# First level of the blockwise inverse in the delta stage: products with the identity become transposes

## What is computed

```python
a_mat = jnp.where(tri_strict, jnp.einsum('bhncd,bhnsd->bhncs', kb, k) * decay, 0.0)
t_mat = a_mat + jnp.eye(C, dtype=a_mat.dtype)
u = lax.linalg.triangular_solve(t_mat, vb, left_side=True, lower=True, unit_diagonal=True)
w = lax.linalg.triangular_solve(t_mat, kb * jnp.exp(g)[..., None], left_side=True, lower=True,
                                unit_diagonal=True)
qk = jnp.where(tri_incl, jnp.einsum('bhncd,bhnsd->bhncs', q, k) * decay, 0.0)

def step(S, xs):
    q_c, k_c, u_c, w_c, qk_c, g_c = xs
    v_new = u_c - jnp.einsum('bhcd,bhde->bhce', w_c, S)
    o = jnp.einsum('bhcd,bhde->bhce', q_c * jnp.exp(g_c)[..., None], S) + jnp.einsum('bhcs,bhse->bhce', qk_c, v_new)
    g_last = g_c[..., -1]
    S = S * jnp.exp(g_last)[..., None, None] + jnp.einsum(
        'bhcd,bhce->bhde', k_c * jnp.exp(g_last[..., None] - g_c)[..., None], v_new)
    return S, o
```

## Time and profile before

| | |
|---|---|
| median of 3 runs | 6135.12 us (6133.20 to 6140.82) |
| span of the profiled execution | 6134.8 us |
| the delta stage in it | about 1560 to 2455 us |
| a head in the loop | 113 us |
| busy over the whole span | PE 44%, DVE 65%, ACT 10%, POOL 52% |

### The profile page before, as it was taken

One profiled execution on the slowest core, in us unless ns is written; L12 is line 12 of the kernel. 1 busy time (PEld: TensorE's weight loads), 2 busy tenths in 40 slices (PEclk: granted clock), 3 DMA queues, 4 the chain that ended last, 5 costly groups with the idle time before them and its releaser, 6 DMA issues. The chain is left out here.

```text
span 6134.8 us, 45197 instructions
## 1 busy us (share of the span) xinstructions
PE 2702.1 (44%) x14507; PEld 2157.5 (35%) x14507; DVE 3964.2 (65%) x4739; ACT 604.5 (10%) x670; POOL 3200.9 (52%) x1475
## 2 busy tenths in 40 slices
PE   6799998978688888789670000000000000000000
PEld 2678886754577676569560000000000000000000
DVE  0234464234465665343588888888888888888888
ACT  0122121213211111111210000000000000000000
POOL 0243223323211211220224888888888888888887
PEclk9699998988899898799885555555555555555555
DMA  6254336440000000242315999999999999999998
GB/s 234 89 199 137 101 130 211 160 152 0 23 9 9 17 9 3 79 166 63 117 48 227 380 384 379 373 398 373 383 379 387 389 392 383 378 383 384 389 376 335
DMA packets 374740, 1384.38 MB, mean 226 GB/s; under 512 B 26927, under 2 KB 203367, under 8 KB 239735
## 3 DMA queue, kind: packets, MB, share of 16 engines
q0 software_dynamic: 147968, 1073.84, 44.3%
q1 hardware_dynamic: 214775, 280.33, 13.7%
q10 hardware_dynamic: 11904, 29.01, 1.2%
HBM read 1352.10 MB, written 31.00 MB: 225 GB/s over the span
## 5 line engine op out<-in xcount | busy, mean ns | idle before, releaser
L2018 DVE SCALAR_TENSOR_TENSOR expert_sum<-expert_rows,expert_acts,expert_sum 128x2048 f32<-128x2048 f32 x512 | 1206.2, 2356 | 211.5 <-DMA expert_rows<-in_peer_v,gather_index 154.2
L2000 DVE CUSTOM_DVE_ANT_0 expert_rows<-expert_rows,h_tile 128x2048 f32<-128x2048 f32 x512 | 1169.0, 2295 | 184.3 <-DMA expert_rows<-in_peer_u,gather_index 160.1
L1973 POOL DMA_INDIRECT expert_rows<-in_peer_v,gather_index x512 | 1124.9, 2197 | 188.6 <-issue 136.8
L1973 POOL DMA_INDIRECT expert_rows<-in_peer_u,gather_index x512 | 1078.5, 2106 | 189.7 <-issue 137.6
L671 POOL TENSOR_TENSOR w_low<-w_raw,w_high 128x2048 fp32r<-128x2048 f32 x76 | 360.4, 4746 | 724.9 <-ACT w_high L552 724.9
L235 PE MATMUL psum<-hT_high,w_high 128*128 128x512 f32 (+1 forms) x1536 | 573.8, 374 | 60.7 <-POOL w_low L671 60.7
L236 PE MATMUL psum<-hT_low,w_high 128*128 128x512 f32 (+1 forms) x1536 | 555.9, 371 | 0.0
L238 PE MATMUL psum<-hT_high,w_low 128*128 128x512 f32 (+1 forms) x1536 | 518.0, 371 | 0.0
L235 PEld LDWEIGHTS psum<-hT_high,w_high 128*128 128x128 f32 x1536 | 292.5, 190 | 135.0 <-POOL w_low L671 52.5
L628 DVE SCALAR_TENSOR_TENSOR mod_sums<-ada_rows,cond_silu,mod_sums 128x1024 f32<-128x1024 f32 x128 | 243.6, 1903 | 108.6 <-DMA ada_rows<-in_ada_w 103.9
L236 PEld LDWEIGHTS psum<-hT_low,w_high 128*128 128x128 f32 x1536 | 292.3, 190 | 49.7
(11 more groups left out here) (311 smaller groups left out, 5614.4 us busy)
## 6 DMA issues: line engine op xcount, KB each, us to landing
w_raw<-in_w_in SPq DMA_DIRECT2D x38, 2048.0 KB, 10.5
ada_rows<-in_ada_w SPq DMA_DIRECT2D x128, 512.0 KB, 5.4
ada_chunk<-in_ada_w SPq DMA_DIRECT2D x16, 2048.0 KB
w_out_chunk<-in_w_out SPq DMA_DIRECT2D x8, 2048.0 KB, 8.9
w_q_raw<-in_peer_w_q SPq DMA_DIRECT2D x16, 1024.0 KB, 5.7
features<-stage ACTq DMA_DIRECT2D x56, 256.0 KB, 2.5
x<-in_w_branch_attn SPq DMA_DIRECT2D x8, 1024.0 KB
x<-in_w_branch_dn SPq DMA_DIRECT2D x8, 1024.0 KB
```

What stands on the lines that cost most here:

```text
L1973: nc.gpsimd.indirect_dma_start(out=ring[:, slot, :], out_offset=None, in_=tables[phase], in_offset=bass.IndirectOffsetOnAxis(ap=idx[:, ban ...
L2000: v.tensor_tensor_reduce(ring[:, b % RING, :], ring[:, b % RING, :], h2s[:, :], 1.0, 0.0, ALU.mult, ALU.add, hid16[:, b:b + 1]).then_inc(u ...
L2018: v.scalar_tensor_tensor(out=y[:, :], in0=ring[:, b % RING, :], scalar=acts[:, ds(i * TURN + b, 1)], in1=y[:, :], op0=ALU.mult, op1=ALU.ad ...
```

## The change

At level 0 both products with the identity are written as `nc.tensor.transpose` of the block: 12 blocks in phase 0 (of `A`) and 12 in phase 1 (of `Y`), in each of 8 heads. Operand in the array, moving operand, PSUM place and semaphore counts are the same. No instruction changes its place on any engine: row by row the order of all five streams is that of before, apart from line numbers, which are 24 lower after the change (line 1135 becomes 1111 or 1114), as blank lines at the head of the file are gone.

```diff
                         for j in range(a, b):
                             m = d * NT + j
                             c = slice((j - a) * P, (j - a + 1) * P)
+                            if n == 0:
+                                mm = nc.tensor.transpose(ps[:, g, c], (A if phase == 0 else Y)[:, m, :], ident)
+                                continue
                             if phase == 0:
-                                mm = nc.tensor.matmul(ps[:, g, c], A[:, m, :], ident if n == 0 else R[:, m, :], start=True, stop=True)
+                                mm = nc.tensor.matmul(ps[:, g, c], A[:, m, :], R[:, m, :], start=True, stop=True)
                                 continue
                             if n < 5:
-                                mm = nc.tensor.matmul(ps[:, g, c], Y[:, m, :], ident if n == 0 else Ti[:, m, :], start=True, stop=True)
-                            if n > 0:
-                                compact = ps[:, g, 2 * P + (j - a) * CHUNK:2 * P + (j - a + 1) * CHUNK].rearrange("p (c b) -> p c b", b=1 << n)
-                                mm = nc.tensor.matmul(compact, Ti[:, m, :], changed(Y[:, m, :], d, n), start=True, stop=True)
+                                mm = nc.tensor.matmul(ps[:, g, c], Y[:, m, :], Ti[:, m, :], start=True, stop=True)
+                            compact = ps[:, g, 2 * P + (j - a) * CHUNK:2 * P + (j - a + 1) * CHUNK].rearrange("p (c b) -> p c b", b=1 << n)
+                            mm = nc.tensor.matmul(compact, Ti[:, m, :], changed(Y[:, m, :], d, n), start=True, stop=True)
                         mm.then_inc(S["inv_pe"], 1)
```

## The result

The changed kernel takes 6172.57 us (median of 4 runs, 6168.79 to 6179.82) against 6137.97 us before (4 runs, 6133.20 to 6142.99). The ratio is 1.0057 with an interval of 1.0043 to 1.0071: slower, clear of noise. 6142 was forecast, with a range from 6126 to 6154. Of the executions behind the table further down, one of the kernel with doubled transposes (9494 us) and one of the kernel before (7041 us) stand far apart from all others and are left out of the ratios.

The account below looks back on a forecast made before the run. Level 0 was ruled by PE's low clock, DVE and POOL, with PE back to back from level 1. Five heads losing 1.8 us, two winning 0.6, head 0 winning 1.3: +6.5 on 6134.8, so 6142 us; range 6126 to 6154.

Parts of the forecast that it names:

- The meeting of that update with POOL: Level 0, phase 1: DVE's SBUF-only update waits for POOL's instruction under way to end, taking 0.9 us or more.
- a clock that stays low into level 1: Halved PE records leave gaps at level 0, so the rise comes in level 1 in five of seven loop heads.
- if the rise comes as long behind the start of level 1 as it came behind s before, 2.9 to 6.2 us: Level 1, delay once counted from the head's first product (s): price 1.5 to 3.1 us a head, 2.2 as a middle.
- rival 2: Clock stays low well into level 1 in all seven heads, 2.5 us each: +17 us, 6151; chance 0.22.
- two where it comes within level 0: Two of seven loop heads whose clock rises within level 0, each winning 0.6 us.
- mark of 3 us: Level 1: a clock rise later than 3 us behind its start was said to outweigh the gain.
- Rival 1: Level 0: clock rises as early as before; heads win 0.5 us on average at level 1, total 6130; chance 0.25.
- Rival 3: Transposes don't raise the clock at all; all eight heads pay 2.2 us: +18, 6153; chance 0.05.
- the prediction's sentence on the page: Skill page says full clock doesn't engage for transposes; by it the last rival but one below would be the forecast.

## Why the prediction was wrong

**What held.** The places of level 0 came out nearly to the record: phase 1 at 4.36 us (4.44 foretold), the first update of line 1317 at 5.08 to 5.09 (5.27), dn_v_new at 7.71 (7.73), level 1 at 10.92 (10.5 to 11.2). The meeting of that update with POOL was right and was shown by holding POOL back. Head 0 won 1.1 us (1.3). That transposes raise the clock as products do, read from the earlier trace rows, was right, and so was the direction of the effect, a clock that stays low into level 1. In the five heads of the first sort the loss was 1.4, 2.7, 1.5, 1.7 and 2.5 us, 2.0 on average (1.8); this is luck in part, since 1.6 us in each of heads 2 and 7 are the second fall of the clock, at the start of combine, which the prediction doesn't have. Without it the average is 1.3.

**The term that failed** is "if the rise comes as long behind the start of level 1 as it came behind s before, 2.9 to 6.2 us". It took level 1 for one dense stretch. In five heads the rise did come in its phase 0, 1.8 to 4.0 us in; in heads 3 and 5 it came 26 us behind the start of level 1. But phase 0 lasts only 8 us at the lower clock and is broken by line 1175, and a head that misses it there went through the 13 us of phase 1 as well, without a rise though PE was back to back (one head of the run with transposes in phase 1 alone did get it there, late). Heads 3 and 5 lost 11.1 and 11.6 us, over four times the 2.5 us of rival 2, and make 23 of the 32 us. That the profile shows PE busy doesn't tell that the clock is up: here it was busy for 35.72 of 37.03 us, at the lower level throughout.

**The count of heads.** The "two where it comes within level 0", with 0.6 us won each, were none. The breaks around line 1175 and the wait for dn_v_new lie in every head, and in none of seven was there a rise in level 0. With the measured sizes the sum is -1.1 + 9.9 + 22.8 = 31.6 us, which is what the stage lost, and would have come to 6166.

**The rivals.** Rival 2 named the mechanism, "the clock stays low well into level 1 in all seven heads", with a chance of 0.22 and 6151 us; its price was too small, for the reason above. Its mark of 3 us doesn't follow from the prediction's own terms: with half a us lost for each us at the lower clock, a gain of 0.4 us is gone 0.8 us behind the start of level 1, and head 2, whose rise came 1.8 us behind it, was slower by 0.8 us already at the end of its inverse. Rival 1 (the rise as early as before) was refuted in all heads of the loop. Rival 3 gave a time nearer the measured one for a cause that the doubled transposes rule out; it is the rival that the prediction's sentence on the page means, where it says the last but one. Not weighed at all was that POOL's place, which shifts the start of level 1 by about 1 us, bears on whether a head waits 37 us, as the run with POOL held back shows. What stays open is why a given head is of one sort or the other.

## What to carry to other kernels

Before taking work off PE in a stretch where it is not the bound, ask whether that work raises or holds its clock for the PE-bound stretch behind it; the saving there was mostly hidden behind DVE and POOL, and the loss was not. The price can hang on another engine: with POOL's work held back the same change cost no time that could be told. Read the granted clock in short stretches, not PE's busy share, and price a late rise up to the end of the next stretch that has raised it before, not by the time it took elsewhere. If the clock is the matter, try to fill PE's idle time up to the start of the stretch and keep the dense form of the work: here that, together with POOL held back, gave 0.3%, where the leaner form alone cost 0.6%.

## What the hardware showed that was not expected

The clock didn't rise in 13 us of PE back to back at level 1, phase 1 (pairs of 128 and 64 columns), in two heads of the changed kernel, nor in nine more of the kernels with half the products (two), with 15 products (three) and with 24 products (four) ahead of the transposes. In all eleven it rose in phase 0 of level 2. In one head of the kernel with transposes in phase 1 alone it did rise there, after 8 us. The reason is open. The clock also fell without a long wait: in a stretch of 6.7 us with 4.76 us busy and a longest wait of 1.94 us, and at the start of combine behind a wait of 0.38 us. A DVE update that touches SBUF alone waited for POOL's instruction to end in every loop head of the changed kernel (0.9 to 1.1 us where it is 0.42 without), and POOL's next grew from 1.05 to 1.23 us in return; moving POOL's work by 8 to 13 us took 6 to 7 us off head 0 alone.
